# Softmax statistics with fewer VectorE operations: negated queries, and the gate applied in GpSimd's scaling of E

## The reference

```python
def masked_softmax(s, mask):
    s = jnp.where(mask, s.astype(jnp.float32), NEG_INF)
    m = jnp.max(s, axis=-1, keepdims=True)
    e = jnp.where(mask, jnp.exp(s - m), 0.0)
    return e / jnp.maximum(jnp.sum(e, axis=-1, keepdims=True), 1e-30)
# q is scaled by dh ** -0.5 (SM in the kernel), dh = 64
return gb[..., 0:1] * o_cmp + gb[..., 1:2] * o_slc + gb[..., 2:3] * o_win
```

## Time and profile before

| | |
|---|---|
| median of 3 runs | 1413.69 us (1413.56 to 1413.87) |
| time of the profiled execution | 1417.01 us |
| its span | 1415.2 us |
| busy share of the span: PE, DVE, ACT, POOL | 96%, 53%, 43%, 50% |
| granted TensorE clock, mean | 0.992 of full speed |

### The profile page before, as it was taken

One profiled execution on the slowest core, in us unless ns is written; L12 is line 12 of the kernel. 1 busy time (PEld: TensorE's weight loads), 2 busy tenths in 40 slices (PEclk: granted clock), 3 DMA queues, 4 the chain that ended last, 5 costly groups with the idle time before them and its releaser, 6 DMA issues.

```text
span 1415.2 us, 17822 instructions
## 1 busy us (share of the span) xinstructions
PE 1359.3 (96%) x6884; PEld 1122.4 (79%) x6884; DVE 750.5 (53%) x1047; ACT 607.7 (43%) x1091; POOL 710.8 (50%) x544
## 2 busy tenths in 40 slices
PE   5999999799999999999999999989999999999998
PEld 4888877577988888888878888766688888888886
DVE  4515658764454445554464075788355544556443
ACT  4224457655533333422352335667454333334322
POOL 1644677664544444444445457677445444445441
PEclk9999999999999999999999999999999999999999
DMA  5333330022232333233233334100214233323331
GB/s 199 107 109 105 108 101 16 1 90 87 82 100 93 102 94 100 90 104 93 72 104 103 108 110 134 36 10 24 96 61 118 91 104 90 105 90 102 91 103 61
DMA packets 34596, 127.19 MB, mean 90 GB/s; under 512 B 3920, under 2 KB 4304, under 8 KB 34128
## 3 DMA queue, kind: packets, MB, share of 16 engines
q1 hardware_dynamic: 34512, 126.05, 28.2%
HBM read 123.94 MB, written 2.10 MB: 89 GB/s over the span
## 4 chain that ended last, share of the span: by engine, by line
PE 86%; DVE 5%; ACT 4%; issue 2%; POOL 1%; DMA 0%; SPq 0%; DVEq 0%; ACTq 0%; POOLq 0%
PE bank L1669 32%; PE bank L1701 17%; PE bank L1337 17%; PE bank L1353 5%; PE bank L1572 3%; PE bank L1606 2%; PE bank L1629 1%; DVE s_bias L1152 1%; PE bank L1630 1%; PE bank L1312 1%; PE bank L1437 1%; PE bank L1522 1%; DVE pt_l L896 1%; POOL w_lo L527 1%; PE bank L1541 1%
## 5 line engine op out<-in xcount | busy, mean ns | idle before, releaser
L527 POOL TENSOR_TENSOR w_lo<-raw,w_hi 128x1024 fp32r<-128x1024 f32 x216 | 519.9, 2413 | 481.3 <-ACT w_hi L622 480.9
L622 ACT ACTIVATE w_hi<-raw 128x1024 fp32r<-128x1024 f32 x220 | 231.0, 1055 | 250.6 <-DMA raw<-wstream 250.3
L1669 PE MATMUL bank<-act_hi,w_hi 128*128 128x512 f32 (+1 forms) x768 | 285.8, 372 | 0.8 <-DVE act_lo L896 0.6
L1669 PE MATMUL bank<-act_hi,w_lo 128*128 128x512 f32 (+1 forms) x768 | 285.2, 371 | 0.0
L1669 PE MATMUL bank<-act_lo,w_hi 128*128 128x512 f32 (+1 forms) x768 | 285.2, 371 | 0.0
L855 ACT ACTIVATE cv<-bank,par 128x512 f32<-128x512 f32 x88 | 68.6, 780 | 286.0 <-PE bank L1669 286.0
L1273 DVE SCALAR_TENSOR_TENSOR cv<-bank,par,cv 128x511 f32<-128x511 f32 x88 | 66.0, 750 | 225.3 <-ACT cv L855 225.3
L1669 PEld LDWEIGHTS bank<-act_hi,w_hi 128*128 128x128 f32 x768 | 144.7, 188 | 26.6 <-DVE act_lo L896 1.0
L1669 PEld LDWEIGHTS bank<-act_hi,w_lo 128*128 128x128 f32 x768 | 144.7, 188 | 25.0
L1669 PEld LDWEIGHTS bank<-act_lo,w_hi 128*128 128x128 f32 x768 | 144.7, 188 | 24.9
L1337 PE MATMUL bank<-w_hi,act_hi 128*128 128x512 f32 (+1 forms) x384 | 146.0, 380 | 6.8 <-DVE w_lo L896 3.6
(11 more groups left out here) (175 smaller groups left out, 2240.7 us busy)
## 6 DMA issues: line engine op xcount, KB each, us to landing
raw<-wstream SPq DMA_DIRECT2D x220, 512.0 KB, 3.6
g_all<-gains SPq DMA_DIRECT2D x2, 2048.0 KB, 7.1
x<-x_in SPq DMA_DIRECT2D x4, 512.0 KB, 7.8
x_out<-x SPq DMA_DIRECT2D x8, 256.0 KB, 2.0
const<-consts SPq DMA_DIRECT2D x1, 1030.0 KB, 14.3
g_all<-gains SPq DMA_DIRECT2D x1, 512.0 KB, 5.1
par<-pars SPq DMA_DIRECT2D x2, 235.0 KB, 3.6
const<-consts SPq DMA_DIRECT2D x1, 224.0 KB, 5.4
```

What stands on the lines that cost most here:

```text
L527: nc.gpsimd.tensor_tensor(w_lo[:, s, :], raw_slot(s), r32(w_hi[:, s, :]), ALU.subtract)\
L622: nc.scalar.activation(w_hi[:, s, :], raw_slot(s), ACT.Copy).then_inc(hi_ready, 1)
L1669: last = mm(bank[:, b, first:end], a, v, start=(k == 0 and n == 0), stop=(k == KD - 1 and n == 2), skip_group_check=True)
```

## The change

The scores are now negated and scaled as they are made. ACT writes the high part of the queries with scale -SM, and DVE writes the low part as -SM times the feature minus the high part. The masks hold +1e30 in place of -1e30. A row's minimum is then the bias itself, and the exponential takes scale -1.0. The second operation on s_bias (L1155) goes.

`factors` goes from DVE. POOL waits for the exponentials themselves, raises the bare sums to -1, and multiplies E by two [P, 1] operands in one TENSOR_SCALAR: the inverse sum, then the gate. POOL waits once a layer for gate_inv.

In the compressed softmax the sum's guard also multiplies by gate_inv, the product with the gate goes, and the product with cE comes one turn sooner (7 steps). The order of what stays is as it was.

```diff
                 def scale(n, p):
-                    pool.wait_ge(r_step, upto(r_step, l, 2 * n + p + 1))
+                    pool.wait_ge(e_done, upto(e_done, l, G * n + 2 * p + 2))
                     nc.gpsimd.tensor_tensor(s_rec[:, n % SB, heads], s_sum[:, n % SB, heads], minus_one[:],
                                             ALU.pow).then_inc(rec_done, 1)
                     for r in (2 * p, 2 * p + 1):
                         e = E[:, slot, r, col:col + P * (i + 1)]
-                        nc.gpsimd.tensor_tensor(e, e, s_rec[:, n % SB, r:r + 1].broadcast_to([P, P * (i + 1)]),
-                                                ALU.mult).then_inc(p_scaled, 1)
+                        weight = 3 * (G * g + r) + b + 1
+                        nc.gpsimd.tensor_scalar(e, e, s_rec[:, n % SB, r:r + 1], gate[:, i, weight:weight + 1],
+                                                ALU.mult, ALU.mult).then_inc(p_scaled, 1)
+                pool.wait_ge(inv_ready, upto(inv_ready, l, 1))
...
-                                             bank[m * DH:(m + 1) * DH, F_BANK[f], :], ACT.Copy).then_inc(q_h, 1)
+                                             bank[m * DH:(m + 1) * DH, F_BANK[f], :], ACT.Copy, scale=-SM)\
...
-                    act.wait_ge(m_step, upto(m_step, l, 2 * z + 2))
+                    act.wait_ge(m_step, upto(m_step, l, z + 1))
-                                             ACT.Exp, bias=s_bias[:, n % SB, r:r + 1], scale=SM,
+                                             ACT.Exp, bias=s_bias[:, n % SB, r:r + 1], scale=-1.0,
...
-                        minus(QS[(1 - m) * DH:(2 - m) * DH, 2 * (f - 4) + m, :], bank[m * DH:(m + 1) * DH, F_BANK[f], :],
-                              r32(QS[m * DH:(m + 1) * DH, 2 * (f - 4) + m, :])).then_inc(q_l, 1)
+                        nc.vector.scalar_tensor_tensor(
+                            out=QS[(1 - m) * DH:(2 - m) * DH, 2 * (f - 4) + m, :],
+                            in0=bank[m * DH:(m + 1) * DH, F_BANK[f], :], scalar=-SM,
+                            in1=r32(QS[m * DH:(m + 1) * DH, 2 * (f - 4) + m, :]), op0=ALU.mult, op1=ALU.subtract)\
...
-                def maxima(z):
+                def minima(z):
-                    nc.vector.reduce_max(bias, bank[:, S_BANK(z), 0:count * width].rearrange("p (q c) -> p q c", q=count),
-                                         AXX).then_inc(m_step, 1)
-                    dve.wait_ge(m_step, upto(m_step, l, 2 * z + 1))
-                    nc.vector.tensor_scalar(bias, bias, NEG_GUARD, -SM, ALU.max, ALU.mult).then_inc(m_step, 1)
+                    nc.vector.tensor_reduce(out=s_bias[:, n % SB, first:first + count],
+                                            in_=bank[:, S_BANK(z), 0:count * width]
+                                            .rearrange("p (q c) -> p q c", q=count), axis=AXX, op=ALU.min)\
+                        .then_inc(m_step, 1)
...
-                def factors(n, p):
-                    dve.wait_ge(e_done, upto(e_done, l, G * n + 2 * p + 2))
-                    nc.vector.scalar_tensor_tensor(out=sums, in0=sums, scalar=1e-30, in1=gs, op0=ALU.max,
-                                                   op1=ALU.mult).then_inc(r_step, 1)
...
                     if n == 3:
-                        nc.vector.tensor_scalar(rec, rec, 1e-30, None, ALU.max).then_inc(c_step, 1)
+                        nc.vector.scalar_tensor_tensor(
+                            out=rec.rearrange("p (t r) -> p t r", t=T), in0=rec.rearrange("p (t r) -> p t r", t=T),
+                            scalar=1e-30,
+                            in1=gate_inv[:].rearrange("p t (g r b) -> p g t r b", g=NKV, b=3)[:, g, :, :, 0],
+                            op0=ALU.max, op1=ALU.mult).then_inc(c_step, 1)
...
-                    if n == 6:
-                        dve.wait_ge(c_step, upto(c_step, l, at + 7))
                         nc.vector.tensor_tensor(cE[:, g], cE[:, g], rec.unsqueeze(2).broadcast_to([P, T * G, NCP]),
                                                 ALU.mult).then_inc(c_step, 1)
...
                 for k in range(NI + 3):
-                    for unit, p in pairs_at(k - 2):
-                        factors(unit, p)
```

More of the change, by code:

```diff
@@ L284, in build @@
         cs_done = sem("cs_done", 2)
-        c_step = sem("c_step", 16)
+        c_step = sem("c_step", 14)
         c_exp = sem("c_exp", 2)
@@ L294, in build @@
         s_done = sem("s_done", len(JOBS))
-        m_step = sem("m_step", 2 * len(JOBS))
+        m_step = sem("m_step", len(JOBS))
         e_done = sem("e_done", G * NU)
-        r_step = sem("r_step", 2 * NU)
         rec_done = sem("rec_done", 2 * NU)
@@ L576, in scale @@
                 def scale(n, p):
-                    i = UNITS[n][0]
+                    i, g, b = UNITS[n]
                     slot, col = E_AT[n]
@@ L745, in queries_first @@
                         nc.scalar.activation(QS[m * DH:(m + 1) * DH, 2 * (f - 4) + m, :],
-                                             bank[m * DH:(m + 1) * DH, F_BANK[f], :], ACT.Copy).then_inc(q_h, 1)
+                                             bank[m * DH:(m + 1) * DH, F_BANK[f], :], ACT.Copy, scale=-SM)\
+                            .then_inc(q_h, 1)
                 act.wait_ge(par_loaded, upto(par_loaded, l, 32))
@@ L828, in _ @@
                         if k == CMP_AT[g] + 1:
-                            act.wait_ge(c_step, upto(c_step, l, 8 * g + 3))
-                            nc.scalar.activation(cE[:, g], cE[:, g], ACT.Exp, scale=SM).then_inc(c_exp, 1)
+                            act.wait_ge(c_step, upto(c_step, l, 7 * g + 3))
+                            nc.scalar.activation(cE[:, g], cE[:, g], ACT.Exp, scale=-1.0).then_inc(c_exp, 1)
                     for z in jobs_at(k - 1):
@@ L1141, in _ @@
                 minus(VcS[:, :, DH:2 * DH], vcf[:], r32(VcS[:, :, 0:DH])).then_inc(vc_l, 1)
-                def maxima(z):
+                def minima(z):
                     n, first, count = JOBS[z]
                     width = P * (UNITS[n][0] + 1)
-                    bias = s_bias[:, n % SB, first:first + count]
                     dve.wait_ge(s_done, upto(s_done, l, z + 1))
@@ L1173, in compressed_first @@
                 def compressed_first(g):
-                    at, b = 8 * g, CMP_BANK[g]
+                    at, b = 7 * g, CMP_BANK[g]
                     rows = bank[:, b, :].rearrange("p (r c) -> p r c", c=NCP)
+                    stat = c_stat[:, g * 16:g * 16 + 16]
                     dve.wait_ge(cs_done, upto(cs_done, l, g + 1))
-                    nc.vector.reduce_max(c_stat[:, g * 16:g * 16 + 16], rows, AXX).then_inc(c_step, 1)
+                    nc.vector.tensor_reduce(out=stat, in_=rows, axis=AXX, op=ALU.min).then_inc(c_step, 1)
                     dve.wait_ge(c_step, upto(c_step, l, at + 1))
-                    nc.vector.tensor_scalar(c_stat[:, g * 16:g * 16 + 16], c_stat[:, g * 16:g * 16 + 16], NEG_GUARD, None,
-                                            ALU.max).then_inc(c_step, 1)
+                    nc.vector.tensor_scalar(stat, stat, -NEG_GUARD, None, ALU.min).then_inc(c_step, 1)
                     dve.wait_ge(c_step, upto(c_step, l, at + 2))
-                    nc.vector.tensor_tensor(cE[:, g], rows, c_stat[:, g * 16:g * 16 + 16].unsqueeze(2)
-                                            .broadcast_to([P, 16, NCP]), ALU.subtract).then_inc(c_step, 1)
+                    nc.vector.tensor_tensor(cE[:, g], rows, stat.unsqueeze(2).broadcast_to([P, 16, NCP]),
+                                            ALU.subtract).then_inc(c_step, 1)
                 for z in range(EARLY):
-                    maxima(z)
+                    minima(z)
                     if z == 3:
                         compressed_first(0)
[L1189 to L1193, removed]
                 queries_rest(6)
-                factors(1, 1)
                 def p_rest(k):
@@ L1216, in compressed_step @@
                 def compressed_step(g, n):
-                    at = 8 * g
+                    at = 7 * g
                     rec = c_rec[:, g * 16:g * 16 + 16]
@@ L1548, in turn_y @@
                         pe.wait_ge(y_step, upto(y_step, l, 8))
-                        pe.wait_ge(c_step, upto(c_step, l, 8 + 3))
+                        pe.wait_ge(c_step, upto(c_step, l, 7 + 3))
                     else:
@@ L1597, in turn_p @@
                         i, g = query_tile(v)
-                        pe.wait_ge(c_step, upto(c_step, l, 8 * g + 8))
+                        pe.wait_ge(c_step, upto(c_step, l, 7 * g + 7))
                         for r in range(G):
@@ L1759, in _constants @@
     out[:, O_ID:O_CA] = np.eye(P, dtype=f)
-    out[:, O_CA:O_CM] = np.where(np.arange(P)[None, :] <= np.arange(P)[:, None], 0, NEG)
+    out[:, O_CA:O_CM] = np.where(np.arange(P)[None, :] <= np.arange(P)[:, None], 0, -NEG)
     tok = np.arange(SEQ).reshape(T, P).T[:, :, None]
@@ L1763, in _constants @@
     out[:, O_II:] = np.tile(np.eye(P // 2, dtype=f), (2, 1))
```

(2 more changed lines are left out.)

8 lines of the change are left out of this document (1 added, 7 removed).

## The result

The changed kernel takes 1404.82 us, the median of 6 runs (1398.92 to 1406.13), beside 1413.78 us for the kernel before in the same comparison (6 runs, 1411.55 to 1418.35). The ratio is 0.9925, with a 95% interval from 0.9902 to 0.9948. It is 9.0 us faster, where 12.2 were forecast. The profiled execution took 1406.13 us with a span of 1404.3 us; 1404.8 us were forecast for it.

A forecast was written before the change was run, and what follows sets the result against it. PE, busy 96%, bounds the kernel, so only its waits for DVE count: 5.6 and 5.4 us a layer, together 11.0, plus 1.2 from the clock, give 1413.7 - 12.2 = 1401.5 us; range 1393 to 1411.

The forecast's parts named there:

- queries, first: PE's 1.3 us wait for the queries: one bias operation goes from their path, 0.2 us gained a layer.
- cE and second query wait: PE's waits of 0.3 and 0.6 us: the cE product comes a turn sooner, four bias operations go; all 0.9 gained.
- pt_l ahead of E's transposes: PE's three waits for DVE's pt_l, 3.6 us in the first layer: 2.9 us gained together.
- turned outputs: PE's three waits for act_lo before the turned retention outputs, 4.4 us: 1.1 us gained together.
- ahead of the projection: PE's 0.9 us wait for act_lo before the projection: two small operations go, 0.3 us gained.
- The other pt_l wait: The 0.3 us PE waits for pt_l beside the large waits: 0.2 us gained.
- The clock: Less PE idle makes falls to half clock rarer: 1.2 us gain, between a loss of 3 and a gain of 8.
- sign of failure: The prediction fails if, among other signs, the half-clock stretches grow past 25 us.
- the new operation: POOL's TENSOR_SCALAR scaling of E, taken at 1.04 us for 512 columns, no gain and no loss.
- the two long ones: DVE operations held by POOL's w_lo near 247 and 283 us; PE's pt_l waits behind them give 1.6 and 1.1 us.
- Given back: Rival: the PE-ACT exchange over pt_h holds the loop, pt_l waits move without shrinking; 1410.7 us, chance 0.11.
- POOL as the bound: Rival: POOL's two-operand scaling costs two passes and exceeds its 28.4 us of waits a layer; 1441 us, chance 0.07.

The follow-up runs named there:

- before_fill: The kernel before with idle products for PE ahead of its waits for queries, second turned output and the stretch's end: 1409.45 us, ratio 0.9965.
- fill_all: The changed kernel with idle products for PE ahead of its waits for queries, second turned output and the stretch's end: 1399.5 us, ratio 0.9914; again 1400.7 us, 0.9895.
- bias_only: The kernel before with the negated queries, masks and minima alone, factors staying on DVE: 1408.53 us, ratio 0.997 to the kernel before.
- gate_only: The kernel before with only the factors moved into POOL's scaling, bias operations staying: 1408.10 us, ratio 0.9964 to the kernel before.
- fill_mid: The changed kernel with idle products ahead of PE's waits for queries and second turned output, none at the tail: 1401.54 us, ratio 0.9904.
- pool_twice: The changed kernel with POOL's scaling of E as two passes, inverse sum then gate: 1451.07 us, ratio 1.0269 to the kernel before.
- dummy_two: The changed kernel with 32 unread operations a layer, two SBUF inputs each, at the factors' old places in DVE's queue: 1408.57 us, ratio 0.9971.

## Why the prediction was right, point by point

**The bound.** That only PE's waits count, and DVE's relief as such does not, held. DVE lost 17 us a layer (14 forecast) and the stretch 4.0 and 5.5.

**The number.** The forecast for the profiled execution was 1404.8 us and 1406.13 were measured, 1.3 more. For the median 2.0 more were missed by taking over the 3.3 us between the profiled execution and the median: they were 3.3 before and are 1.3 after. Such a difference is one execution's place in the spread, and no constant.

**The waits.** 11.0 us were forecast for both layers, 11.4 measured at equal clock by the length of the stretches (before_fill against fill_all). Single terms of the first layer, by the waits of the earlier trace rows and those of after:

| term | forecast | measured |
|---|---|---|
| queries, first (with E's 0.5) | 0.2 | -0.1 (1.8 to 1.9) |
| cE and second query wait | 0.9 | 0.5 (0.9 to 0.4) |
| pt_l ahead of E's transposes | 2.9 | 2.9 (3.6 to 0.7) |
| turned outputs | 1.1 | 1.3 (4.4 to 3.1) |
| ahead of the projection | 0.3 | 0.2 (0.9 to 0.7) |

The other pt_l wait, 0.3 us in the trace of before with 0.2 forecast of it, is gone from the rows too. In all, PE's waits fell by 5.1 us in the first layer and 4.3 in the second (5.6 and 5.4 forecast), leaving out the wait at the tail that the low clock hides. So the sum over both layers came a little short by the waits and a little over by the length at full clock, and the agreement of 11.0 with 11.4 is closer than the single terms are. The query path itself did get 0.2 us shorter: from the last reduce to PE it was 203.32 to 207.61, and is 201.36 to 205.46; PE comes to it earlier, so its wait does not show that.

**The clock.** This is the step that failed, in sign: "I take 1.2 us of gain". Its size follows from the profiled executions. From the chain of work, the two stretches are 270.9 us long in all before and 261.0 after, 9.9 us apart. With the fillers and the full clock it is 11.4. So the falls take back 1.5 us where 1.2 were to be given. Before, the clock was low for 3.4, 3.4 and 10 us in these stretches; after, for 3.4, 3.4, 6.8, 3.4 and 6.8, which is 23.8 us in all and close to the 25 that the prediction named as a sign of failure. The long one of the second layer shrank with the idle ahead of it, as argued, and two new ones came at the tail, at 1.7 us each, for which the prediction had no term beyond its bound of 3 us of loss. PE idles there as it did before (1.87 us in both). Why a fall comes there now stays open; bias_only and gate_only have it in both layers, and in fill_mid it came in one layer and not in the other.

**POOL.** 1.04 us were taken for the new operation at 512 columns, 0.77 measured, within the bounds of 0.61 and 2.08. As forecast, it set no limit: PE has no wait for E in the changed kernel. The estimate made from the Trainium skill (GPSIMD Engine Reference, Engine selection; 0.62 us at 512 columns) was low by 0.15: the slope of 0.84 ns a column is nearly the 1/1.2 = 0.83 of that estimate, and the missing part is the fixed cost, 0.35 us in place of 0.19.

**The holds.** They are real, and only operations with all inputs in SBUF show them. But the prediction priced the two long ones as if each belonged to its operation. bias_only shows that a hold passes to the next such operation in the queue. gate_only shows that it also depends on when w_lo starts: with POOL free of DVE's queue the two-column bias operation is held for 0.58 us in place of 1.74, and the 1.1 us of PE's wait behind it are gone while the operation stays. So this term came out as forecast, but the 1.1 us go with the factors (0.83 are left in bias_only, none in gate_only), and not with the bias operation to which they were put down.

**The rivals.** Given back did not happen, since the pt_l waits shrank and did not move. POOL as the bound is what pool_twice shows, 39 us above the kernel before where 27 were given.

## What to carry to other kernels

Look for operations of VectorE whose inputs all lie in SBUF next to long GpSimd operations; remove all of them at such a place, for the hold goes to the next one, and see when the GpSimd operation starts, for that sets how long the hold is. Price a relief by the waits of the engine that sets the end, each by its own path, and not by the relieved engine's busy time. When such waits shrink by some us, expect the clock of TensorE to fall at other places, compare at equal granted clock, and try idle products inside the waits: here they were worth 1.5 to 5 us on top of the change, by the ratios (0.9914 and 0.9895 beside 0.9925 and 0.9931).

## What was not expected of the hardware

A kernel's runs spread by up to 10 us (bias_only, 1405.4 to 1415.4), most of it with the granted clock (0.987 to 0.999 over all runs but those of pool_twice). In these traces the low stretches last 3.4, 6.8 or 10 us, the last in the kernel before and in dummy_two. GpSimd's TENSOR_SCALAR with two [P, 1] operands has a larger fixed cost than its TENSOR_TENSOR with a spread operand (0.35 against 0.19 us). It is the slower one at 128 columns and the quicker one at 256 (559 against 617 ns); an estimate from the two lines puts the crossing at some 190: 0.19 + 0.00167 n = 0.35 + 0.00084 n gives n = 193.
